# One core, SSD branch of a hybrid trunk: the causal mask as a matmul, state scaling on GpSimd, the decay-times-CB product on VectorE

## What is computed

```python
seg = a_cs[..., :, None] - a_cs[..., None, :]
decay = jnp.exp(jnp.where(causal, seg, -jnp.inf))
cb = jnp.einsum('bclgn,bcsgn->bcgls', cm, bm)
y_diag = jnp.einsum('bcgls,bcgjls,bcsgjp->bclgjp', cb, decay, xdt)
...
def step(s, inp):
    dec, st = inp
    return dec[..., None, None] * s + st, s
```

## Time and profile before

| | |
|---|---|
| median of 3 runs | 1851.03 us (1849.75 to 1852.66) |
| profiled execution | 1850.61 us, its span 1849.0 us |
| TensorE busy | 1635.9 us (88%) |
| VectorE busy | 729.7 us (39%) |
| ScalarE busy | 413.0 us (22%) |
| GpSimd busy | 264.6 us (14%) |
| mean granted TensorE clock | 0.957 |

### The profile page before, as it was taken

The page is one execution under the profiler, slowest core; times in us unless marked ns, Lnnn a source line. Parts: engine busy times, 40 slices in busy tenths (PEclk is TensorE's granted clock), DMA queues, the critical chain, the costliest instruction groups (busy, mean ns, idle before and its releaser), DMA issues. The chain is left out here.

```text
span 1849.0 us, 23337 instructions
## 1 busy us (share of the span) xinstructions
PE 1635.9 (88%) x9042; PEld 872.5 (47%) x9043; DVE 729.7 (39%) x1304; ACT 413.0 (22%) x769; POOL 264.6 (14%) x287
## 2 busy tenths in 40 slices
PE   4998798799789769999999999999999958999893
PEld 2554454354445334544545545444656434555451
DVE  2545644664654564700016766214025122222124
ACT  4332323233233232000013332410110111111112
POOL 0004402412330440000000000000000012222122
PEclk9998999899899989999999999999989969999997
DMA  9710101011021016712111100214340656998994
GB/s 348 293 46 1 46 23 46 32 37 46 1 91 46 1 49 244 253 46 93 46 46 45 46 18 28 91 46 153 138 181 1 227 224 231 393 343 290 393 385 155
DMA packets 106755, 241.24 MB, mean 130 GB/s; under 512 B 5481, under 2 KB 15214, under 8 KB 106690
## 3 DMA queue, kind: packets, MB, share of 16 engines
q1 hardware_dynamic: 86800, 180.60, 27.1%
q0 software_dynamic: 14288, 48.96, 7.4%
q10 hardware_dynamic: 5602, 10.78, 1.6%
HBM read 218.31 MB, written 22.02 MB: 130 GB/s over the span
## 5 line engine op out<-in xcount | busy, mean ns | idle before, releaser
L439 PE MATMUL psum<-arena 128*128 128x512 f32 x688 | 302.8, 596 | 10.6 <-ACT arena L1279 4.4
L439 PEld LDWEIGHTS psum<-arena 128*128 128x128 f32 x688 | 128.6, 190 | 168.2 <-issue 160.9
L1075 PE MATMUL psum<-arena 128*32 128x256 f32 x2816 | 165.5, 387 | 1.6 <-DVE arena L2193 1.5
L453 PE MATMUL psum<-arena 128*128 128x512 f32 x352 | 155.4, 601 | 1.6 <-issue 1.6
L627 PE MATMUL psum<-arena 128*128 128x512 f32 x256 | 124.9, 626 | 1.0 <-ACT arena L1319 1.0
L1075 PEld LDWEIGHTS psum<-arena 128*32 128x32 f32 x2816 | 91.9, 111 | 60.0 <-issue 7.0
L764 PE MATMUL psum<-arena 128*128 128x512 f32 x256 | 111.5, 593 | 0.0
L453 PEld LDWEIGHTS psum<-arena 128*128 128x128 f32 x352 | 67.3, 193 | 84.0 <-issue 83.7
L2301 POOL TENSOR_TENSOR arena<-arena 128x512 f32<-128x512 f32 x64 | 84.2, 1327 | 131.9 <-ACT arena L1374 131.9
L1729 DVE SCALAR_TENSOR_TENSOR arena<-arena 128x772 f32<-128x772 f32 (+1 forms) x96 | 93.9, 978 | 3.4
L2271 POOL TENSOR_TENSOR arena<-arena 128x512 f32<-128x512 f32 x40 | 46.5, 1174 | 336.1 <-ACT arena L1319 282.1
(11 more groups left out here) (363 smaller groups left out, 2122.8 us busy)
## 6 DMA issues: line engine op xcount, KB each, us to landing
arena<-exp_w_d SPq DMA_DIRECT2D x48, 2048.0 KB, 17.3
arena<-w_in_d SPq DMA_DIRECT2D x22, 2048.0 KB, 7.9
arena<-ada_w_d POOLq DMA_DIRECT2D x8, 2048.0 KB, 9.3
slots<-arena POOLq DMA_DIRECT2D x1, 9216.0 KB, 27.1
arena<-ada_w_d SPq DMA_DIRECT2D x4, 2048.0 KB, 21.5
arena<-ssd_proj_d SPq DMA_DIRECT2D x4, 2048.0 KB, 9.8
slots<-arena POOLq DMA_DIRECT2D x92, 64.0 KB, 4.9
arena<-slots POOLq DMA_DIRECT2D x22, 256.0 KB, 6.0
```

Of the source, the lines that this page charges most:

```text
L439: ins = mmul(ps[:, 0:T], slot[:, k, m * P:(m + 1) * P], src[:, k, C:NT], start=(k == 0), stop=(k == KD - 1))
L453: ins = mmul(ps[:, 0:n], src[:, k, t * P:(t + 1) * P], slot[:, k, 0:n], start=(k == 0), stop=(k == KD - 1))
L1075: ins = mmul(psU[q * R:(q + 1) * R, 0:2 * HF], XT[:, k % 2, k // 2, :], w13[p][:, :, k, q * HF:(q + 1) * HF], start=(k == 0), stop=(k == K ...
```

## The change

- The masks move to TensorE. `cb` becomes one unmasked copy. A bf16 tile `shut[d]` holds 0 where a decay counts and -1e30 where it doesn't, and `rows_of` adds it in PSUM with a second matmul (L646 of the changed kernel), before the exponential.
- The subtraction in `exponents` becomes one `tensor_tensor` over 512 elements, without the clamp.
- The product of the decays with CB moves from GpSimd to VectorE (`decay`), one or two heads behind the subtraction.
- The scaling of the old state moves from VectorE to GpSimd (`scale_state`, buffer `Send`), three for each direction; with the products gone, `make_xw` and `make_xdt` of the backward direction stand in a plain row.
- One z matmul moves from before the last x transposes to after them: two z matmuls now stand between `x_turn` and `first_state`.
- The four forward spreads of group g+1 move from its state stage into the second y stage of group g, on TensorE and on ScalarE.
- The squares of y are summed after all four `finish` instead of between them. Small preparations (`d_col`, the epsilon) move to the front.

```diff
-        cb = [alloc(TL, P) for _ in range(2)]
+        cb = alloc(TL, P)
+        Send = alloc(GW)
+        shut = [tmpd[0].rearrange("p t h -> p (t h)")[:, 0:P].bitcast(BF16)[:, d * P:(d + 1) * P] for d in range(2)]
-        Z_FRONT = 11
-        Z_STATES = (3, 3, 3, 2, 2)
+        Z_FRONT = 10
+        Z_STATES = (3, 3, 2, 2, 2)
...
-                    ins = mmul(ps[:, :], selb[0:3 * SH, hh:hh + 1].to_broadcast([3 * SH, P]),
-                               rowsT[0:3 * SH, d, :], start=True, stop=True)
+                    mmul(ps[:, :], selb[0:3 * SH, hh:hh + 1].to_broadcast([3 * SH, P]),
+                         rowsT[0:3 * SH, d, :], start=True, stop=False)
+                    ins = mmul(ps[:, :].rearrange("p (c l) -> p c l", c=TL), identb,
+                               shut[d].unsqueeze(1).to_broadcast([P, TL, P]), start=False, stop=True)
...
+                z_part(2)
                 first_state(0, 4, 8)
                 for i in range(2, 6):
                     for b in range(2):
-                        spread((i - 2) // 2, (i - 2) % 2 * 2 + b)
+                        if g == 0 or i >= 4:
+                            spread(g, (i - 2) // 2, (i - 2) % 2 * 2 + b)
...
                             for i in range(2 * b + 2, min(2 * b + 4, 7)):
                                 next_part(g + 1, i)
+                            if g < SG - 1:
+                                spread(g + 1, 0, b)
...
+                        if d and g < SG - 1 and h in (3, 5, 7):
+                            spread_out(g + 1, 0, (h - 3) // 2)
...
-                            step(v.tensor_tensor(heads(vtmp), heads(S[(i - 1) % 2]), per_head(eend), ALU.mult))
-                            ins = v.tensor_tensor(S[i % 2], vtmp, bank(key)[:, :], ALU.add)
+                            dve.wait_ge(S_("S_scaled"), (g * 2 + d) * 3 + i - 1)
+                            ins = v.tensor_tensor(S[i % 2], Send, bank(key)[:, :], ALU.add)
...
-                    for c in range(TL):
-                        ins = v.tensor_scalar(mm[n % NM][:, c, :], bank(key)[:, c * P:(c + 1) * P],
-                                              acs[:, TC + c, at:at + 1], 0.0, ALU.subtract, ALU.min)
-                    ins.then_inc(is_free(key)[0], 1)
+                    v.tensor_tensor(mm[n % NM], bank(key)[:, :].rearrange("p (c l) -> p c l", c=TL),
+                                    acs[:, TC:TT, at:at + 1].to_broadcast([P, TL, P]), ALU.subtract).then_inc(is_free(key)[0], 1)
...
+                def decay(d, h):
+                    n = (g * 2 + d) * HPG + h
+                    dve.wait_ge(S_("decay_ready"), n + 1)
+                    v.tensor_tensor(mm[n % NM], mm[n % NM], cb, ALU.mult).then_inc(S_("M_ready"), 1)
...
+                def scale_state(d, i):
+                    pool.wait_ge(*is_free(("kv", g, d, i - 1)))
...
+                make_xw(0, 0)
+                make_xw(0, 1)
+                for i in range(2, 5):
+                    make_xw(0, i)
+                    scale_state(0, i)
```

More of the change, by code:

```diff
@@ L1361, in _, with spread_out @@
                 xtok_evac(3)
-                for d in range(2):
+                def spread_out(g, d, b):
+                    key = ("E", g, d, b)
+                    act.wait_ge(*is_full(key))
+                    run(E[d][:, b, :], bank(key)[:, :], ACT.Exp).then_inc(is_free(key)[0], 1)
+                if g == 0:
                     for b in range(HPG // 2):
-                        key = ("E", g, d, b)
-                        act.wait_ge(*is_full(key))
-                        run(E[d][:, b, :], bank(key)[:, :], ACT.Exp).then_inc(is_free(key)[0], 1)
+                        spread_out(0, 0, b)
                 for d in range(2):
@@ L1369, in _ @@
                         z_silu(1)
+                        for b in range(HPG // 2):
+                            spread_out(g, 1, b)
                         z_silu(2)
@@ L1680, in _ @@
                     .then_inc(S_("hT_ready"), 1)
+            dve.wait_ge(S_("rows_in"), 16)
+            step(v.memset(small[:, 62:63], EPS))
+            step(v.tensor_copy(d_col[0:SHD, :], r_("ssd_d")[0:SHD, 0::2]))
+            step(v.tensor_copy(d_col[SHD:P, :], r_("ssd_d")[SHD:P, 1::2]))
             for i in range(2):
@@ L1747, in _ @@
             dve.wait_ge(S_("consts_in"), 16 * 2)
+            for d in range(2):
+                v.tensor_scalar(shut[d], mask[d], -1.0, 1e30, ALU.add, ALU.mult)
             step(v.tensor_copy(identb, ident))
@@ L1787, in _ @@
                 dve.wait_ge(*is_full(key))
[L1788 to L1795, removed]
-                ins.then_inc(is_free(key)[0], 1)
+                v.tensor_copy(cb, bank(key)[:, :].rearrange("p (c l) -> p c l", c=TL)).then_inc(is_free(key)[0], 1)
                 conv(g, "x", 2)
@@ L1866, in _ @@
                 exponents(0, 1)
-                for i in range(1, 4):
-                    state_step(1, i)
-                    exponents(0, i + 1)
+                state_step(1, 1)
+                exponents(0, 2)
+                decay(0, 0)
+                decay(0, 1)
+                state_step(1, 2)
+                exponents(0, 3)
+                decay(0, 2)
+                state_step(1, 3)
+                exponents(0, 4)
+                decay(0, 3)
                 exponents(0, 5)
+                decay(0, 4)
                 state_step(1, 4)
                 exponents(0, 6)
+                decay(0, 5)
                 state_step(1, 5)
                 exponents(0, 7)
-                for h in range(4):
+                decay(0, 6)
+                decay(0, 7)
+                exponents(1, 0)
+                for h in range(1, 6):
                     exponents(1, h)
-                for b in range(2):
-                    exponents(1, 2 * b + 4)
-                    exponents(1, 2 * b + 5)
-                    finish(b)
+                    decay(1, h - 1)
+                finish(0)
+                for h in range(6, 8):
+                    exponents(1, h)
+                    decay(1, h - 1)
+                finish(1)
+                decay(1, 7)
                 finish(2)
                 finish(3)
+                for b in range(3):
+                    add_square(g, b)
             add_square(SG - 1, 3)
             dve.sem_inc(S_("ssum_ready"), 1)
-            v.memset(small[:, 62:63], EPS).then_inc(S_("eps_set"), 1)
             for s in range(4, 12):
@@ L2295, in _ @@
                 make_xw(1, 1)
[L2296 to L2307 removed]
+                for i in range(2, 5):
+                    make_xw(1, i)
+                    scale_state(1, i)
+                for b in range(HPG // 2):
+                    make_xdt(1, b)
             pool.wait_ge(*is_full(("y", SG - 1)))
```

28 lines of the change are left out of this document (7 added, 21 removed).

## The result

The changed kernel takes **1857.78 us** (median of 12 runs, 1854.37 to 1860.44); the kernel before took 1851.30 us beside it (12 runs). The ratio is 1.0033, with a 95% interval of 1.0022 to 1.0043: slower by 0.2 to 0.4%. The forecast was no change, 1850.

A forecast was written before the change was run, and what follows sets the result against it. The prediction took TensorE, busy 88% of the span, plus its idle as the bound. Terms of -25.6, +20.7, +2.5 and +1.5 summed to -0.9 on the profiled 1850.6, giving 1850 us, range 1834 to 1866.

The forecast's parts named there:

- state stages: Each group's stretch from the last x transposes to the first `rows_of`: 25.6 us less over four groups.
- first y stages: Each group's stretch from the first `rows_of` to that of d = 1: 44.8 us a group, +20.7 in all.
- second y stages: Each group's stretch from the `rows_of` of d = 1 to the next group's projection: +2.5 us in all.
- start of group 1: B evacuation some 1.4 us later in group 1, where x waits for the C evacuation: +1.5 us.
- chain: Dependent steps and waits of one first y stage, added by their prices: 39.2 us at 2.4 GHz.
- 3.5 spells at 1.6: First y stage: TensorE falls to 1.2 GHz after near-idle stretches, 3.5 times at 1.6 us, 5.6 us a group.
- The first y stage stays at 1.2 GHz: Slower rival: idle holds the clock down over turns 1 and 2, 4 us a group more, 1866 us; chance 0.24.
- The clock holds: Faster rival: new waits of 2.3 to 3.2 us are harmless, only the last costs, 1834 us; chance 0.25.
- Engine choice alone: Faster rival: VectorE's quicker product removes the 39.4 us of waits, masks cost 14, 1799 us; chance 0.03.

The follow-up runs named there:

- run with its waits filled: Changed kernel with useless bf16 mask matmuls filling most of TensorE's waits in the first y stage, order kept: 1827.80 us.
- run filled ahead of `kv`: Changed kernel with useless matmuls only before `kv` in turns 0 to 2, the waits before y left unfilled: 1843.98 us.
- run with products 0 and 1 alone ahead: Changed kernel with VectorE's products 0 and 1 before the first backward state step, other turns as in the change: 1837.27 us.

## Why the prediction was wrong

The prediction summed -25.6 (state stages), +20.7 (first y stages), +2.5 (second y stages) and +1.5 (start of group 1) to -0.9. Measured in the branch: -26.6, +34.0, +2.1 and, for the start of group 1, +0.9; the projections of groups 2 and 3 add -1.7, which the sum did not have.

**State stages: right in size, by two errors that nearly cancel.** 24.88 against 25.0, and three times about 22.75 against 23.1. Their clock is 1.00, and the long waits for GpSimd and for the state add are gone, as foreseen (0.4 us and, once, 0.6 are left). But the 22.75 hold one z matmul more, 0.86 us, that came in from the front and that the prediction entered at 0; the work it did count came out 1.2 below its 23.1 (the four spreads that left were 1.1 and not 0.9, for one).

**First y stages: the chain right, the clock wrong.** The step that failed reads: "I take 3.5 spells at 1.6: 5.6, so 44.8 a group." The run with its waits filled has 39.2 us at a clock of 1.00, as the chain said, and the changed kernel has 48.1. So this term is 8.9 and not 5.6, and over four groups that is 13.3 us, the whole error (9.6 in the branch) and somewhat more. The prediction had named stages over 48 us as a sign that it is wrong, and three of the four were (48.07, 48.96 and 48.90). Two things were too low. The price of a spell: 1.6 us was the delay of y and z together behind one wait in the kernel before, where z took 2.69. In the new turns z takes up to 3.8. From start to start in group 0, y, z and `rows_of` lose 1.6, 3.0, 1.7 and 2.6 us in turns 0 to 3 (turn 0: 4.49 us from y to the first `rows_of` behind z, where full clock has 2.85), 2.2 on average. And the number: all four turns had a spell, 4 x 2.2, which is the 8.9. The waits themselves were foreseen: 2.9 us ahead of `kv` in turn 0 against 3.2 in the prediction, 2.6 and 2.3 ahead of y in turns 1 and 2 against 2.8 and 2.3, and 3.7 against 3.8 in turn 3. (The terms that the prediction lists for turn 3 add to 36.1 and not 36.3; 36.3 was measured.)

**The rivals.** "The first y stage stays at 1.2 GHz", 1866 with a chance of 0.24, came nearest in size: it was 4 us a group beyond the spells counted, and 3.3 came. Its mechanism is not what the trace shows. The clock was not held down over turns 1 and 2; `off` and `kv` ran at full speed there, and y, z and `rows_of` fell again behind each long wait. (Its work of 5.4 us a turn is some 5.7 by the earlier trace rows.) "The clock holds" fell: state stages had kept their clock behind waits of up to 2.7 us, which said little about a stage with such a wait in each turn. "Engine choice alone", 1799, named a gain that is there, and more (1783), once the queue's order lets it through. I had read from the order that it would not come in this change, and that held. The products beside GpSimd's scalings took 2.75 us for two, as priced: they end 7.1 and 8.5 us after the first `rows_of`, where the chain has 7.3 and 8.7.

**Second y stages: right.** 23.8 against the 23.7 foreseen, 19.67 against 20.

**Start of group 1: right in kind.** The wait for the C evacuation grew from 4.4 to 5.7 us (+1.3), and the projections of group 1 took 68.44 us against 67.54 (67.8 to 69.0 over the variants with the same wait). The fronts of groups 2 and 3 became 0.86 shorter each (61.22 to 60.36, 62.44 to 61.58). That is the z matmul that went from each front into the state stage; the prediction had entered it at 0 in both places. In group 1 the same 0.86 goes off the delay, which is 1.8 without it, against the 1.5 foreseen. Together with the state stages this hid a part of the clock's error.

What stays open: why a wait of the same length let the clock fall in most turns and not in some (2.60 us in group 3 of the run filled ahead of `kv`, 3.72 us in group 0 of the run with products 0 and 1 alone ahead). No run here separates that from where in time the wait falls.

## What to carry to other kernels

An operation that moves to a faster engine takes a place in that engine's queue, and the place can cost more than the engine gives: the same product on VectorE cost 48 us in one order and gained 26 in another, against GpSimd. Put what the next matmul of the chain needs first (here the state step), and right behind it the work for the next turn, so that it is done before that turn's state step comes. Where TensorE waits in each turn of a loop as long as here (2.3 to 3.7 us), count the work behind each wait at half clock rather than at the price of a spell seen elsewhere. By that estimate y and z (2.85 us at full clock) cost 2.85 more in each turn; 1.6 to 3.0 was measured, 2.2 on average. Filling the waits with useless matmuls tells in one run how much of a stage is the clock.

## What the runs showed of the hardware

- Useless work made the kernel 30 us faster: 44 bf16 matmuls in each group, 9.7 us of TensorE at about 0.22 each, brought the clock of the stage from 0.76 to 0.82 up to 1.00 and its length from 48.1 to 39.2 us.
- In the changed kernel the clock fell in all 16 turns of the first y stages, which take 7.6 to 9.4 us each at full clock, each time behind a wait of 2.3 to 3.7 us. In the kernel before, one wait of 2.7 us in a state stage had left it at 1.00 in two of four; and in two of the variants it stayed up behind single waits of 2.60 and of 3.72 us. The Trainium skill (TensorE: Matmul & The Clock Gate, "HAM oscillation — how this bites in real kernels") tells of a matmul kernel that waits for a DMA in each step and starts every step cold. The four slow z of one stage are the same pattern, with VectorE in the DMA's place, though here the first matmul behind the wait often still ran at full speed (y 1.10 us in turn 2).
- One VectorE product of 128x512 takes 0.68 us alone and up to 1.5 beside GpSimd's operations, on data in SBUF; the subtraction, which reads PSUM, stayed at 0.68 to 0.69 in all 64 instances, also while GpSimd worked (at 163.39 above).
